# The next chunk's convolution tail, layer norm and attention issued between the feed-forward slots, in an unrolled program

## The reference

```
h    = rmsnorm(x)
proj = h @ w_in                       # 2560 columns: conv value, gate, q, k, v (512 each)
u    = a * sigmoid(gate)
c    = dwconv31(u) + b_dw             # causal, depthwise, 512 channels, 31 taps
c    = silu(layernorm(c)) @ w_pw      # 512 x 512
q, k = rmsnorm per head (8 x 64)
o    = stick_breaking(q, k, v)        # A[t,s] = beta[t,s] * prod_{s<j<t}(1 - beta[t,j]), s < t
x    = x + concat(c, o) @ w_out       # 1024 x 1024
x    = x + relu(rmsnorm(x) @ w_ff1)^2 @ w_ff2    # 1024 -> 4096 -> 1024
```

## Time and profile before

| | us |
|---|---|
| median of three runs | 3403.99 (3400.26 to 3405.33) |
| profiled execution, first to last instruction | 3399.0 |
| PE busy | 2901.9 (85%) |
| DVE busy | 1896.1 (56%) |
| POOL busy | 1435.7 (42%) |
| ACT busy | 1236.9 (36%) |

### The profile page before, as it was taken

One profiled execution on the slowest core, in us unless ns is written; L12 is line 12 of the kernel. 1 busy time (PEld: TensorE's weight loads), 2 busy tenths in 40 slices (PEclk: granted clock), 3 DMA queues, 4 the chain that ended last, 5 costly groups with the idle time before them and its releaser, 6 DMA issues.

```text
span 3399.0 us, 39340 instructions
## 1 busy us (share of the span) xinstructions
PE 2901.9 (85%) x13936; PEld 2376.3 (70%) x13936; DVE 1896.1 (56%) x2447; ACT 1236.9 (36%) x1992; POOL 1435.7 (42%) x784
## 2 busy tenths in 40 slices
PE   7768899997667899997677789999776777899999
PEld 5546777786456777785455677778654666788887
DVE  6965322258786322258789622224885998333333
ACT  3254222332464322332455422233235665322221
POOL 5443344444543444444533334444453443333332
PEclk9977999998889999998888899999897998899999
DMA  5333323332422333331412233334233221222221
GB/s 176 112 106 99 115 89 99 99 130 65 152 87 81 114 90 99 99 130 66 164 66 74 65 108 99 87 87 129 84 109 110 75 80 37 87 81 86 74 74 53
DMA packets 275071, 325.91 MB, mean 96 GB/s; under 512 B 14177, under 2 KB 199521, under 8 KB 272925
## 3 DMA queue, kind: packets, MB, share of 16 engines
q1 hardware_dynamic: 274973, 324.64, 30.3%
HBM read 280.17 MB, written 44.43 MB: 95 GB/s over the span
## 4 chain that ended last, share of the span: by engine, by line
PE 59%; DVE 25%; issue 7%; ACT 4%; POOL 4%; DMA 1%; DVEq 0%; SPq 0%; ACTq 0%; POOLq 0%
DVE cacc L1045 10%; PE ps L1326 8%; PE ps L1328 8%; PE ps L1327 8%; PE ps L1602 7%; PE ps L1603 7%; PE ps L1604 7%; DVE stay L1215 4%; DVE aT_lo L351 3%; PE ps L1531 2%; PE ps L1564 1%; POOL w_lo L595 1%; PE ps L1566 1%; PE ps L1565 1%; DVE mixT_hi L1240 1%
## 5 line engine op out<-in xcount | busy, mean ns | idle before, releaser
L702 POOL TENSOR_TENSOR w_lo<-w_raw,w_hi 128x1024 fp32r<-128x1024 f32 x224 | 544.1, 2461 | 753.3 <-ACT w_hi L716 753.3
L716 ACT CAST w_hi<-w_raw 128x1024 fp32r<-128x1024 f32 (+1 forms) x384 | 373.5, 1031 | 624.9 <-PE ps L1604 507.1
L1326 PE MATMUL ps<-hT_hi,w_hi 128*128 128x512 f32 (+1 forms) x1600 | 570.0, 356 | 36.1 <-DVE uT L1085 23.6
L595 POOL TENSOR_TENSOR w_lo<-w_raw,w_hi 128x1024 fp32r<-128x1024 f32 (+1 forms) x160 | 407.3, 2571 | 452.4 <-ACT w_hi L716 452.4
L1327 PE MATMUL ps<-hT_lo,w_hi 128*128 128x512 f32 (+1 forms) x1600 | 567.9, 355 | 0.0
L1328 PE MATMUL ps<-hT_hi,w_lo 128*128 128x512 f32 (+1 forms) x1600 | 567.5, 355 | 0.0
L679 POOL TENSOR_TENSOR beta<-beta,stay 128x127 f32<-128x127 f32 (+4 forms) x200 | 290.1, 1451 | 483.5 <-DVE stay L1215 483.5
L1303 DVE TENSOR_TENSOR resid<-ps,resid 128x512 f32<-128x512 f32 (+1 forms) x272 | 188.1, 691 | 522.4 <-PE ps L1604 522.4
L1602 PE MATMUL ps<-w_hi,hid_hi 128*128 128x512 f32 (+1 forms) x1088 | 431.4, 397 | 17.0 <-DVE hid_lo L1294 17.0
L1288 DVE TENSOR_TENSOR fsq<-frel 128x512 f32<-128x512 f32 (+1 forms) x160 | 164.3, 1028 | 492.9 <-ACT frel L984 492.0
L1045 DVE SCALAR_TENSOR_TENSOR cacc<-uT,vecs,cacc 128x512 f32<-128x512 f32 (+1 forms) x480 | 436.7, 962 | 3.7
(11 more groups left out here) (128 smaller groups left out, 4847.4 us busy)
## 6 DMA issues: line engine op xcount, KB each, us to landing
w_raw<-in_w_ff SPq DMA_DIRECT2D x256, 512.0 KB, 4.1
w_raw<-in_w_in SPq DMA_DIRECT2D x80, 512.0 KB, 4.0
w_raw<-in_w_out SPq DMA_DIRECT2D x32, 512.0 KB, 3.9
a_q<-q_scratch SPq DMA_DIRECT2D x33, 256.0 KB, 5.1
a_q<-q_scratch SPq DMA_DIRECT2D x66, 128.0 KB, 5.0
xin<-in_x_prompt SPq DMA_DIRECT2D x16, 512.0 KB, 5.2
resid<-in_x_prompt SPq DMA_DIRECT2D x16, 512.0 KB, 6.0
v_scratch<-vpack SPq DMA_DIRECT2D x16, 512.0 KB, 3.6
```

The costliest lines, as they stand in the source:

```text
L595: nc.gpsimd.tensor_tensor(w_lo[g % 2][:, j, 0:width], w_raw[:, j, 0:width], w_hi[g % 2][:, j, 0:width].bitcast(F32), ALU.subtract).then_in ...
L702: nc.gpsimd.tensor_tensor(w_lo[g % 2][:, j, :], w_raw[:, j, :], w_hi[g % 2][:, j, :].bitcast(F32), ALU.subtract).then_inc(lo_done, 1)
L716: nc.scalar.copy(w_hi[g % 2][:, j, 0:width], w_raw[:, j, 0:width]).then_inc(hi_done, 1)
L1326: nc.tensor.matmul(out, w[0], x[0], start=start, stop=False)
```

## The change

Stages 3 and 4 of chunk c+1 are no longer stages: they are issued inside the feed-forward of chunk c. The order is now ag, kvq of chunk c+1, then a `window` that holds ff(c) together with the rest of the taps, layer norm, pw and attention of c+1, then out(c+1). The first window holds no feed-forward, the last one holds nothing else. `window` counts slots: 128 for chunks 0 to 2 (eight rounds of 16: eight half blocks of w_ff1, then eight half tiles of w_ff2, 12 matmuls each). Slots 0 to 13 carry two taps each (`LATE`, 28 taps), 14 to 25 the layer norm, then pw, and from slot 31 (39 for the last chunk) to 115 the attention steps, spread evenly: 73, 105 and 154 steps for the second, third and fourth chunk. `EARLY` falls to 11 and the share of a k or q tile rises to 2, which leaves 63 taps in kvq.

Attention pieces are 128 queries by at most 512 keys now; where a piece continues another, DVE copies one column (L1353) and POOL multiplies all of it, in place of the one-column product L1214. The squared relu is taken in PSUM. Attention and pw results go to memory and come back as `mixT` (1 MB a transfer, four of them) over the space of the feed-forward's input, once its last w_ff1 block is done. The norm of the next chunk moves from the feed-forward's end into out, and its input is loaded there.

Weights are still fetched raw and split anew: 376 slabs through a ring of eight, in which the raw slab lies where its lo part will. When SP loads a slab and when ACT and POOL split it is set by a table of estimated ticks; ACT and POOL call `splits_until` at the head of each slot. No hardware loops are left.

```diff
+def slots_an_e(c):
+    return 8 + 2 * len(tiles(c))
+LN0 = 14
+LN_STEPS = 12
+def pw_slot(c):
+    return LN0 + LN_STEPS + (8 if c == NC - 1 else 0)
+def att_first(c):
+    return pw_slot(c) + CB + 1
+def att_past(c):
+    return att_first(c) + att_steps_total(c) if c == 0 else 116
+def window_slots(c):
+    return att_past(0) if c < 0 else FFE * slots_an_e(c)
+def att_steps(c, slot):
+    a, b, n = att_first(c), att_past(c), att_steps_total(c)
+    if slot < a or slot >= b:
+        return range(0)
+    return range(n * (slot - a) // (b - a), n * (slot - a + 1) // (b - a))
...
+def ticks():
+    at, t = {}, 0.0
+    for c in range(NC):
+        for a in range(8):
+            at["ag", c, a] = t
+            t += 2
+        for s in range(3 * len(tiles(c))):
+            at["kvq", c, s] = t
+            t += 2
+        for s in range(window_slots(c - 1)):
+            at["win", c - 1, s] = t
...
+def load_tick(n):
+    return use_of(n - RING)[1] if n >= RING else -8.0 + 1.5 * n
+SPLIT_LAG = 2.5
+def split_tick(n):
+    return max(min(load_tick(n) + SPLIT_LAG, use_of(n)[0] - 2.0), -8.0)
...
-        EARLY = 19
+        EARLY = 11
+        LATE = 2 * LN0
...
-            share = [3 if sec == "v" else 1 for sec, i, m in kvq_events(c)]
-            rest, total = TAPS - 3 * EARLY, sum(share)
+            share = [3 if sec == "v" else 2 for sec, i, m in kvq_events(c)]
+            rest, total = TAPS - 3 * EARLY - LATE, sum(share)
...
+            at = {"split": 0}
+            def splits_until(t):
+                while at["split"] < len(W) and split_tick(at["split"]) <= t:
+                    n = at["split"]
+                    pool.wait_ge(hi_done, n + 1)
+                    nc.gpsimd.tensor_tensor(w_s[:, n % RING, SLAB:2 * SLAB], w_raw[:, n % RING, SLAB:2 * SLAB],
+                                            w_s[:, n % RING, 0:SLAB].bitcast(F32), ALU.subtract).then_inc(lo_done, 1)
+                    at["split"] += 1
...
-                with pool.Fori(0, FFE - 1) as e:
-                    for g in (G_FF + 1, G_FF + 2):
-                        for j in range(4):
-                            n = 4 * (GROUPS * c + g) + 8 * e + j
-                            pool.wait_ge(hi_done, n + 1)
-                            nc.gpsimd.tensor_tensor(w_lo[g % 2][:, j, :], w_raw[:, j, :],
-                                                    w_hi[g % 2][:, j, :].bitcast(F32), ALU.subtract).then_inc(lo_done, 1)
-                if c + 1 < NC:
...
+            def att(c, step):
+                q = att_piece(c, step, 1)
+                if q:
+                    n = q.n - 1 if q.diag else q.n
+                    v = beta[q.z % 4]
+                    pool.wait_ge(s_scan, q.z + 1)
+                    if not q.diag:
+                        pool.wait_ge(s_edge, q.z - q.m + 1)
+                    nc.gpsimd.tensor_tensor(v[0:q.r, 0:n], v[0:q.r, 0:n], stay[q.z % 3][0:q.r, 1:n + 1],
+                                            ALU.mult).then_inc(s_a, 1)
+            def window(c):
+                for s in range(window_slots(c)):
+                    splits_until(TICK["win", c, s] + 2)
+                    if c + 1 < NC:
+                        for n, step in ln_step(c + 1, s):
+                            ln(c + 1, n, step)
+                        for step in att_steps(c + 1, s):
+                            att(c + 1, step)
...
+                for s in range(window_slots(c)):
+                    splits_until(TICK["win", c, s] + 2)
+                    e, pos = s // se, s % se
...
+                    group = None
+                    if c >= 0 and pos < 8 and (ns == 2 or pos % 2):
+                        group = pos if ns == 2 else pos // 2
+                        j, (s0, w) = group // ns, sp_[group % ns]
+                        f = 4 * FFE * c + 4 * ns * e + group
+                        bank = ps[:, ff_bank(c, e, group), 0:w]
+                        act.wait_ge(f1_ps, f + 1)
...
+                        nc.scalar.activation(hid_f[x][:, j, s0:s0 + w], bank, ACT.Relu).then_inc(f_rel, 1)
+                    for step in steps[:1]:
+                        att_sigmoids(n, step)
+                    if group is not None:
+                        act.wait_ge(f_sq, f + 1)
+                        nc.scalar.copy(hid_hi[x][:, j, s0:s0 + w], bank).then_inc(f_hi, 1)
+                    for step in steps[:1]:
+                        att_later(n, step)
+                    for step in steps[1:]:
+                        att_sigmoids(n, step)
+                        att_later(n, step)
...
+                        if 0 <= s - pw_slot(n) - 1 < CB:
+                            pw(n, s - pw_slot(n) - 1)
+                    steps = att_steps(n, s) if n < NC else range(0)
+                    if s == 0 and n < NC:
+                        dve.wait_ge(consts, 6)
...
+                        bank = ps[:, ff_bank(c, e, group), 0:w]
+                        dve.wait_ge(f_rel, f + 1)
+                        nc.vector.scalar_tensor_tensor(out=bank, in0=bank, scalar=0.0, in1=hid_f[x][:, j, s0:s0 + w],
+                                                       op0=ALU.max, op1=ALU.mult).then_inc(f_sq, 1)
+                    if c >= 0 and pos >= 8:
+                        ev = pos - 8
+                        i, hf = ev // 2, ev % 2
+                        r = tl[i][1]
+                        dve.wait_ge(f2_ps, 8 * FFE * c + 2 * nt * e + ev + 1)
+                        v = resid[0:r, i, hf * BANK:(hf + 1) * BANK] if i < 4 else rsample[0:r, 0, hf * BANK:(hf + 1) * BANK]
+                        nc.vector.tensor_tensor(v, ps[0:r, ff_bank(c, e, 4 * ns + ev), :], v, ALU.add).then_inc(f2_add, 1)
+                    for step in steps[:1]:
+                        att_mask(n, step)
+                    if group is not None:
+                        dve.wait_ge(f_hi, f + 1)
+                        nc.vector.tensor_tensor(hid_lo[x][:, j, s0:s0 + w], bank, hid_hi[x][:, j, s0:s0 + w].bitcast(F32),
+                                                ALU.subtract).then_inc(f_lo, 1)
+                    for step in steps[1:]:
+                        att_parts(n, step)
+                        att_mask(n, step)
...
+                if c:
+                    sp.wait_ge(f1_ps, 4 * FFE * c)
+                for ev in range(2):
+                    sp.wait_ge(pw_st[ev], 16 * (CB * (c + len(conv_pieces(c)))) // 2)
+                if c == NC - 1:
+                    sp.wait_ge(z_ps, att_end(c, "z"))
+                for b in range(2):
+                    if b:
+                        sp.wait_ge(o_st, 16 * att_end(c, "o"))
+                    for v in range(2):
+                        sp.dma_start(mixT[x][v][:, 4 * b:4 * b + 4, 0:n].bitcast(F32),
+                                     mix_d[v, 4 * b:4 * b + 4, :, t0:t0 + n].rearrange("b p t -> p b t")).then_inc(mix_in[b], 16)
```

2091 lines of the change are left out of this document (1101 added, 990 removed).

## The result

The changed kernel takes 3408.77 us (median of 20 runs, 3399.67 to 3412.44), the one before 3402.91 (20 runs): a ratio of 1.0014, 95% interval 1.0008 to 1.0021: 6 us slower, less than 0.2%. Forecast were 3170 us, in a range from 3035 to 3370. The profiled execution's span is 3405.0 us against 3399.0, where my sum came to 3164: 241 us have to be found.

A forecast was written before the change was run, and what follows sets the result against it. The prediction took PE as the engine to fill, with attention running at DVE's pace. Its terms: 3399 - 308 + 103 + 20 - 81 + 31 = 3164, with 5 us added 3169, forecast as 3170 us, range 3035 to 3370.

The forecast's parts named there:

- Term A: Chunks two to four: attention, layer norm and pw hidden under the feed-forward, 790 us of stages becoming 482, gain 308 us.
- the port: In the windows: VectorE with two SBUF inputs and GpSimd reading SBUF exclude each other; no bound in the forecast sum.
- the batch: At each round's turn: four w_ff2 splits in a row delay the product beta; PE waits 3.8, 5 and 4.8 us.
- Term B: In the three windows: waits behind splits (68 us) and in-order engine collisions add 103 us to PE's path, bounds 0 and 240.
- the second rival: In the attention slots: DVE and POOL exclude each other, their work is serial and becomes the bound; 3372 us, chance 0.15.
- Term D: In ag and kvq: fewer DVE taps there save 81 us over four chunks, bounds 30 and 110.
- Term C: In out: waiting for the next chunk's input costs 20 us for the third and fourth chunk, bounds -10 and 40.
- Term E: In the first window, with nothing to hide it: taps and attention's way through memory cost 31 us, bounds 20 and 50.
- The third rival: At every turn of a round: PE has no slack, the splits' waits come through in full; 3474 us, chance 0.08.

The follow-up runs named there:

- The version with 8 columns: Changed kernel with weight splits spread over each round and POOL subtracting only 8 columns of each w_ff1 and w_ff2 slab: 3143.99 us, 0.9247 of the kernel before.
- the spread alone: Changed kernel with the feed-forward's weight splits spread over a round instead of one after the other behind each turn: 3293.42 us, 0.9673 of the kernel before.

## Why the prediction was wrong

*Term A was right in its mechanism.* With the port and the batch out of the way the windows take 1582 us, against 1890 for the same stages before: 308 us, as in the sum. (The version with 8 columns still multiplies as many times.) That it comes out to the microsecond is luck: PE still stands for 55 us in these windows, where term A had it wait for nothing new, and its busy time at full clock is some 1506 us.

*Term B was mis-sized, and this is half of the miss:* 227 us in place of 103, inside the bounds of 0 and 240 that I gave and then left aside. For the batch its mechanism was the right one, and the trace shows the waits where the prediction put them, at the turns: 19, 31 and 47 us in the three windows, where the sum had 19, 25 and 24. Two things made the term dearer. I priced the clock at full speed, while waits of several microseconds are followed by matmuls at the lower one (0.75 in the slice behind the turn above); slow clock takes 101 us in the three windows, not all of it B's.

And the step that failed: I took the exclusion of DVE and POOL for a rival to the batch, to be added only if the pair became the bound, and put it at nothing in the sum. By the sign that I gave for that rival, windows as long as DVE's and POOL's busy times together, that rival seems to hold in one of three: 278 + 237 in 513 us, 350 + 277 in 576, 438 + 316 in 718. But the sign misleads. The two are busy at once for 133, 174 and 201 us and both idle for 131, 123 and 166, and with the splits spread the same work fits in 104 us less. So it is no bound. I read it as a tax on the latency of each step, since the scan stands in a chain of sigmoid, scan, product and transpose that PE meets every 3 us. The forecast had 103 us here and the second rival 306; what was measured lies between, and the port has 97 to 121 of it. The rows named for the rival, had shown the exclusion already.

*A wait that was in no term (most of it is part of the 227):* hid_lo, 65.7 us. DVE has two late taps a slot in the first 14 slots of a window and the layer norm in the next 12, beside squares, low parts and adds; I added up DVE's work over the window, where it fits, and not over its first two rounds, where beside the splits it does not.

*Term D: -35 in place of -81.* The step that failed counted the v tiles' 13 taps less in full and the k and q tiles' 9 more as a quarter, and had nothing for the end of the stage. The kvq matmuls end sooner, by 15.3, 13.5, 19.2 and 0.7 us in the four chunks. But from the last of them to the first matmul of the next stage it is 24.5, 19.2, 22.8 and 15.3 us now, where it was 12.3 to 12.9: 31 of the missing 46 us. There the last q tiles run through their chain, with more taps between its links than before and with the first w_ff1 splits beside them. With 8 columns and the spread that end takes 17.5, 16.6 and 15.4 us in the last three chunks, against 26.6, 26.1 and 17.7 with the spread alone, so the splits have a part in it; how much the taps have was not tried. In ag only 1 to 4 us a chunk went for the first three (11 in the last): it takes 45.9 us now in the second and third, of which 44 are matmuls (192 x 0.229).

*Term C: +53 in place of +20.* The 11.5 us of wait for the input were as forecast (12.0 in the trace). But the first out has 11 us more as well, and taking the wait away brought 9.6 and 5.7 us. The rest of out's loss was not tried.

*Term E: +56 in place of +31.* Taps (18.4 us to the first pw matmul) and the way through memory (13.0 us from the last value matmul to out) came as forecast. In addition attention itself, from the first transpose to the last value, takes 92 us in place of 74, and the stretch from pw to that transpose 8.6 more, at a clock of 0.65 in the whole window. The loads of keys are not the cause (3 us when their waits went); what is, was not found.

*The third rival* did not come: PE never stood 15 us at a turn. The result is outside the range all the same, since B, C, D and E all erred to one side (C and E past their bounds of 40 and 50, B and D just inside theirs): 124 + 33 + 46 + 25, with 8 at the start and 4 at the end, make 240 of the 241.

## What to carry to other kernels

When work is laid under another engine's matmuls, price the latency of the chain that they meet in and not the busy time of its engines: the sum fitted everywhere, and 227 us went. Check such a sum over each round and not over the window alone. Spread what two in-order engines have to do at a point where several buffers come free at once, and keep GpSimd's two-input work on SBUF away from VectorE's. And work that is redone in each pass is worth storing when the DMA engines are two thirds idle; here that took 114 us off, where the change as made took none.

## What the runs showed that was not expected

The scan, whose second input is a broadcast column, pays at the port too: 1.27 us alone, 2.14 beside POOL. A batch costs much of its price even when the slow engine's part is gone: with four casts of 1.05 us left in ACT's row at a turn it still took 74 us of three windows, where it took 104. And reordering PE's attention steps made the kernel slower both times, by 12 and 38 us; the waits for aT_lo grew both times, and why was not shown further.
